# Down weights of the experts issued by the scalar engine instead of the sync engine

## The reference

```
def run_block(args):                       # one block of tokens of one expert
    idx, e, w = args
    xb = x_pad[idx]                        # gather the tokens' normed rows
    hb = silu(xb @ w_gate[e]) * (xb @ w_up[e])     # 1024 -> 256, twice
    return (hb @ w_down[e]) * w[:, None]           # 256 -> 1024, times the routing weight
...
out = out.at[buf_tok].add(yb)              # each token sums its two experts' rows
```

## Time and profile before

| | us |
|---|---|
| median of 3 runs | 1040.3 |
| lowest and highest | 1039.41, 1044.34 |
| the profiled execution's own time | 1038.75 |
| its span, first to last instruction | 1036.7 |

### The profile page before, as it was taken

The page is one execution under the profiler, slowest core; times in us unless marked ns, Lnnn a source line. Parts: engine busy times, 40 slices in busy tenths (PEclk is TensorE's granted clock), DMA queues, the critical chain, the costliest instruction groups (busy, mean ns, idle before and its releaser), DMA issues.

```text
span 1036.7 us, 11829 instructions
## 1 busy us (share of the span) xinstructions
PE 950.2 (92%) x4614; PEld 657.7 (63%) x4614; DVE 478.8 (46%) x980; ACT 306.3 (30%) x512; POOL 198.9 (19%) x172
## 2 busy tenths in 40 slices
PE   6789999999999999899999999994999978876795
PEld 6568778878877876788888874452555434432442
DVE  5538758757955986943333311252211111111543
ACT  3223424445244344722222201121122111111333
POOL 0131326226233531000000000002233322211000
PEclk9989999999999999999999999997999999999798
DMA  6212121032121110432222129389999999995600
GB/s 227 81 61 82 41 102 61 21 119 65 41 86 57 52 40 1 181 164 91 92 98 100 77 90 397 122 312 348 408 420 420 420 419 422 424 413 221 277 40 40
DMA packets 29510, 184.91 MB, mean 178 GB/s; under 512 B 6140, under 2 KB 6524, under 8 KB 19088
## 3 DMA queue, kind: packets, MB, share of 16 engines
q1 hardware_dynamic: 24336, 175.76, 43.0%
q0 software_dynamic: 5120, 8.41, 2.2%
HBM read 175.75 MB, written 16.78 MB: 186 GB/s over the span
## 4 chain that ended last, share of the span: by engine, by line
PE 79%; DMA 13%; DVE 5%; ACT 1%; issue 1%; SPq 0%; ACTq 0%; POOLq 0%; DVEq 0%
PE bank L935 75%; DMA arena<-in_w_expert 8%; DMA yT<-in_w_expert 3%; PE bank L1277 1%; PE bank L1202 1%; DMA mT<-normed,table 1%; PE bank L1034 1%; DVE hT_parts L1414 1%; PE bank L963 1%; DMA arena<-expert_rows 0%; PE bank L1295 0%; DVE yT L1614 0%; DVE arena L1561 0%; DMA x_sb<-in_x 0%; DVE low_parts L1419 0%
## 5 line engine op out<-in xcount | busy, mean ns | idle before, releaser
L935 PE MATMUL bank<-mT_parts,low_parts 128*128 128x512 f32 x448 | 178.4, 398 | 0.0
L935 PE MATMUL bank<-arena,cst 128*64 128x256 f32 (+3 forms) x944 | 142.5, 438 | 16.4 <-DMA arena<-in_w_expert 10.9
L935 PE MATMUL bank<-arena 128*128 128x64 f32 (+7 forms) x592 | 154.0, 401 | 3.9 <-DVE arena L1685 1.7
L935 PE MATMUL bank<-mT_parts,x_parts 128*128 128x512 f32 x320 | 131.2, 410 | 10.7 <-DVE low_parts L1419 10.7
L935 PEld LDWEIGHTS bank<-arena 128*128 128x128 f32 (+1 forms) x592 | 91.3, 189 | 58.8 <-issue 49.2
L935 PE MATMUL bank<-hT_parts,x_parts 128*128 128x512 f32 x320 | 128.2, 401 | 0.0
L1419 DVE TENSOR_TENSOR low_parts<-arena,x_parts 128x1024 fp32r<-128x1024 f32 (+1 forms) x44 | 62.8, 1428 | 116.4 <-ACT x_parts L635 96.6
L935 PEld LDWEIGHTS bank<-arena,cst 128*64 128x64 f32 (+2 forms) x944 | 67.4, 142 | 76.9 <-issue 32.0
L1794 DVE TENSOR_TENSOR cst<-bank,chn 128x512 f32<-128x512 f32 x32 | 22.1, 692 | 196.1 <-PE bank L1277 196.1
L1469 DVE SCALAR_TENSOR_TENSOR arena<-arena,chn 128x512 f32<-128x512 f32 x116 | 99.2, 912 | 0.0
L935 PEld LDWEIGHTS bank<-mT_parts,low_parts 128*128 128x128 f32 x448 | 85.5, 191 | 20.7
(11 more groups left out here) (250 smaller groups left out, 1359.0 us busy)
## 6 DMA issues: line engine op xcount, KB each, us to landing
arena<-in_w_expert SPq DMA_DIRECT2D x24, 2048.0 KB, 26.0
arena<-in_w_expert SPq DMA_DIRECT2D x20, 1024.0 KB, 28.9
arena<-in_w_cm SPq DMA_DIRECT2D x32, 512.0 KB, 3.6
arena<-in_w_gate SPq DMA_DIRECT2D x8, 1536.0 KB, 6.7
x_sb<-in_w_expert SPq DMA_DIRECT2D x8, 1024.0 KB, 29.8
yT<-in_w_expert SPq DMA_DIRECT2D x4, 2048.0 KB, 25.8
hT<-in_w_expert SPq DMA_DIRECT2D x4, 2048.0 KB, 28.0
arena<-in_w_tm SPq DMA_DIRECT2D x4, 1536.0 KB, 7.4
```

The costliest lines, as they stand in the source:

```text
L935: return pe.matmul(out, lhsT, rhs, start=start, stop=stop)
```

## The change

In SP's loop the two lines that wait for `down_done` and issue the down weights are gone, so SP issues up weights only. ACT issues the down weights of expert m+7 right behind its scaling of expert m's rows, the expert whose region they fill. ACT's program order is what protects the region; there is no added wait. The down weights of experts 0 to 6 stay with SP.

```
@@ SP @@
                 if n + 1 < NEXP:
                     sp.wait_ge(up_done, n + 2 - RING)
                     up_weights(n + 1)
-                sp.wait_ge(down_done, n + 1 - RING)
-                down_weights(n)
@@ ACT @@
                 if n:
                     m = n - 1
                     scale_rows(m, m % 2, m % ROWS, m // ROWS * 16 if m >= ROWS else None)
+                    if m + RING < NEXP:
+                        act.dma_start(down_w[m % RING], w_expert[m + RING, :, 4096:6144]).then_inc(we_loaded[m % RING], 16)
```

## The result

| | before | changed |
|---|---|---|
| median, us | 1040.66 (4 runs) | 1056.53 (4 runs) |
| lowest and highest, us | 1039.41, 1044.34 | 1053.66, 1058.98 |
| profiled execution, us | 1038.75 | 1058.98 |
| its span, us | 1036.7 | 1057.1 |

The ratio is 1.0146, with a 95% interval of 1.0109 to 1.0182. The change makes the kernel 16 us slower.

A forecast was written before the change was run, and what follows sets the result against it. The loop was taken as bound by PE first, then by full DMA engines from about 830 to 936 us. Nineteen experts at 8.7 us, five at 6.36 and an 8.7 us tail add 19 us: 1059 us, range 1038 to 1068.

The forecast's parts named there:

- SP loses its issues, ACT gains them, both at nothing: Experts' loop: moving 25 issues gains nothing on SP and costs nothing on ACT, 0.33 us each, hidden by 1.29 us idle.
- The rival of stalls on ACT: Loop: ACT's issues take up to 6.17 us, losing 2 to 3 us on some nine experts: +20, 1060 us; chance 0.05.
- A third queue takes a third turn: DMA engines in the loop: three queues go packet for packet, a turn costs 1.00 us, ten POOL packets 10.0 us.
- The rival without a third turn: Loop: SP's and ACT's transfers share turns or POOL keeps every second; 1040 us, give or take 3; chance 0.22.
- The gathers starve: Loop: POOL's gathers land in 14 to 20 us instead of 9.2; PE waits for them from expert 6 or 7.
- The start of the backlog: Loop: expert 5's gather lands after 13.8 us, about at its limit; each further expert adds 3.6 us.
- The size: Loop: 8.7 us an expert for 19 experts from expert 7, PE's pace afterwards; loop ends at 970.1 us, 19 us later.
- the 9.1: Loop, upper pace per expert: 8 full turns of 8.0 us plus 2 POOL packets at 0.54 us; +26.
- The last weights behind the embedding's: Loop's end: last down weights share turns with x and embedding weights, at most +6, 1046 us; rival, chance 0.08.
- A better tail: Loop's end: early down weights let expert 30 start sooner, 1 to 6 us gained, 1037 us; rival, chance 0.05.

The follow-up runs named there:

- run 1: Changed kernel with ACT also issuing the up weights of experts 7 to 31, so all the loop's weights share ACT's queue: 1045.1 us, ratio 1.0055 to the kernel before.
- run 5: As run 1, but SP issues the first piece of x and the embedding's weights only when expert 29 is done: 1042.87 us, ratio 1.0040 to the kernel before.
- run 8: Changed kernel with every down transfer on ACT cut into two of half the columns, rows of 4 KB: 1052.33 us, ratio 1.0140 to the kernel before.
- run 2: Changed kernel without the gathers of experts 4 to 31: 1028.23 us, ratio 0.9884 to the kernel before.
- run 3: Kernel before the change, without the gathers of experts 4 to 31: 1026.62 us, ratio 0.9875 to the kernel before.
- run 4: Changed kernel with every up transfer on SP cut into two of half the columns, rows of 8 KB: 1040.11 us, ratio 1.0009 to the kernel before.
- run 9: Kernel before the change, with each expert's down weights issued ahead of the next expert's up weights on SP: 1036.34 us, ratio 0.9977.

## Why the prediction was right

It forecast 1059 us for the median, and 1056.5 was measured; for the profiled execution about 1058, and it took 1058.98.

- *SP loses its issues, ACT gains them, both at nothing.* Right: 0.33 us each beside the scaling. ACT's issue starts with the scaling and not behind it, so the down weights weren't even the 1.0 us late that had been allowed for. Even where ACT's issues became long, in runs 1 and 5, the loop lost nothing by them; in run 8, with two issues for each expert, PE waited 1.9 us for ACT. The rival of stalls on ACT is out for this kernel.
- *A third queue takes a third turn.* Right: 1424, 1419 and 1525 packets in 80 us. The rival without a third turn is out.
- *The gathers starve.* Right, and shown from both sides: without them (runs 2 and 3) and with cheap turns (run 4) the loss disappears. The first late gather was that of expert 6, where 6 or 7 had been said. The start of the backlog was overstated: 13.8 us had been worked out for the gather of expert 5, which has 13.6 us and wasn't late, and 3.6 us more for each that follows, but PE waited only 0.94 us for expert 6. Later it was understated: 14 to 20 us to landing had been said, and the gather of expert 12 took 22.1 us.
- *The size.* The pace was 8.52 us an expert, against 8.7 taken and ends of 8.24 and 9.1. The sum behind the 9.1 counted 8 turns for a transfer of weights. There are 9: the 25 down transfers have 3600 packets on 16 engines, 9 for each, one of them small. POOL so gets 9 of its 10 packets beside them. The same sum then gives 8 x 0.93 + 9 x 0.07 + 0.54 = 8.6 us, an estimate made after the result, and nearer to it than the middle that was taken. Expert 7 started at 768.7 us and not at 764.3, because the loop itself began 1.1 us later and two gathers were late by then. The first makes 3.4 us less, the second 4.4 us more; the end of the loop, forecast at 970.1 us, came at 970.9. That the two errors cancel is luck. The median moved by 16 us and the profiled execution by 20. The latter was the slowest of the four, so that it matches the sum to 1 us is luck too.
- *The last weights behind the embedding's.* Right that the changed kernel is spared. Run 1 shows it where the weights aren't early: the wait ahead of expert 29 is 5.7 us there, 1.7 us before, and the run took 5.9 us more than the kernel before, against at most 6.
- *A better tail.* It needed gathers that aren't hurt. Run 4 has them and gained nothing that can be measured; run 9 got 2.5 us by the order within one queue.

The sentence of the Trainium skill that issuing from several engines only saves issue time ("DMA: Bandwidth & Descriptors", section "Issuing engines are not separate DMA queues") doesn't hold here: the same bytes from one more engine cost 16 us. The same page's section "Queues, rings and completion order", by which SP and ACT have rings of their own that are served in turn, agrees with the packet counts.

Still open: the time between a gather's issue and its landing when three queues are full was read off PE's waits, not measured by itself; how soon the weights landed in the changed kernel, which was to be under 41 us, was not measured; the 3.6 us by which leaving out the gathers gained more than their bytes say; and whether the 5.2 us of slower matmuls cost time, or would have been spent waiting for gathers instead.

## What to carry to other kernels

Moving an issue to another engine opens another queue, and queues that hold work share the DMA engines packet for packet, not byte for byte. So before transfers with long rows get a second queue, count the packets that the small, urgent transfers need per step, and multiply by one row of every other queue; if that exceeds the step, they starve although the bandwidth is the same. Count the same for the bulk queues: short rows in one of them beside long rows in another make it the starved one, as in run 8. Put what may be late behind what is urgent in one queue, or keep rows short where queues must meet.

## What the runs showed of the hardware

- Engines serve three full queues packet for packet, with rows of 16 KB and 8 KB beside POOL's packets of 1.7 KB on average (2.61 MB in 1525 packets), and with rows of 16 KB and 4 KB in run 8. A transfer of 128 rows counts 9 packets on each engine, its 8 rows and a small one.
- The stall of a long issue is a matter of the queue and not of the engine that issues: 6.17 us on SP in the earlier trace rows, 5.3 us on ACT in run 1. With fewer transfers in each of two queues there was none: in the changed kernel every issue in the loop took 0.33 to 0.38 us. In run 4, with each up transfer cut in two, SP's longest took 12.6 us, and the run was no slower than the kernel before.
- PE's clock: in the changed kernel, some waits for gathers were followed by slow matmuls and some weren't. After 2.90 us of waiting at 793.33 us `turn_block` took 1.12 instead of 0.66 us and the next 24 matmuls 4.66 instead of 3.66. After the same 2.90 us at 811.57 us nothing was slow. The granted clock is 1.00 from 780 to 790 us and from 810 to 820 us, and 0.83 in the stretch that holds the first of the two waits:

```profile
790.00:800.00 10.00, 7.10 (x42) 3.31 (x39) 1.18 (x3) 1.24 (x3) 1.47 (x2) 0.83 1.01 420
```

```profile
811.57 0.66 PE L1277 MATMUL bank<-cst,mT 128*128 128x128 f32 x4 [2.90 <-DMA mT<-normed,table]
```

  0.83 is a part of the stretch at 1.2 GHz, the lower of the two levels. PE waited for a gather again at its next turn (1.10 us at 802.28 us), and that gather had been issued before the slow matmuls, so the lost microsecond wasn't on the path there. What it did to later gathers isn't shown.
